# The softmax of a sliding-window attention in another order: upper parts before scaling, lower parts before scaling, biases one at a time

## The reference

```python
# first_block and the gMLP half of second_block come before; the part that the change touches:
def swa_mixer(h, k, v, w_in, sinks, w_out):
    q, z = jnp.split(h @ w_in, 2, axis=-1)
    q = q * (HEAD_DIM ** -0.5)
    ...
    dist = BLOCK + r - c
    in_window = (dist >= 0) & (dist < WINDOW)
    alibi = -slopes[:, :, None, None] * dist.astype(jnp.float32)
    def block_fn(args):
        ...
        logits = jnp.einsum('btkgd,bskd->bkgts', qb, kb).astype(jnp.float32) + alibi
        logits = jnp.where(valid, logits, -jnp.inf)
        m = jnp.maximum(jnp.max(logits, axis=-1), sink)
        p = jnp.exp(logits - m[..., None])
        denom = jnp.sum(p, axis=-1) + jnp.exp(sink - m)
        o = jnp.einsum('bkgts,bskd->btkgd', p.astype(vb.dtype), vb).astype(jnp.float32)
        return (o / denom.transpose(0, 3, 1, 2)[..., None]).astype(h.dtype)
    out = lax.map(block_fn, (jnp.arange(n_blocks), q_blocks))
    ...
    y = out * jax.nn.silu(z)
    return y @ w_out
```

## Time and profile before

| | us |
|---|---|
| median of 3 runs | 912.27 |
| lowest, highest | 911.54, 913.71 |
| profiled execution | 914.38 |
| span of its instructions | 912.6 |
| TensorE busy | 880.9 |
| GpSimd busy | 556.2 |
| VectorE busy | 548.0 |
| ScalarE busy | 357.8 |

### The profile page before, as it was taken

The page is one execution under the profiler, slowest core; times in us unless marked ns, Lnnn a source line. Parts: engine busy times, 40 slices in busy tenths (PEclk is TensorE's granted clock), DMA queues, the critical chain, the costliest instruction groups (busy, mean ns, idle before and its releaser), DMA issues.

```text
span 912.6 us, 11943 instructions
## 1 busy us (share of the span) xinstructions
PE 880.9 (97%) x4224; PEld 731.4 (80%) x4224; DVE 548.0 (60%) x878; ACT 357.8 (39%) x792; POOL 556.2 (61%) x620
## 2 busy tenths in 40 slices
PE   8999999999999989999999999999968999998997
PEld 6888888888888877888888888888848888776776
DVE  6125657774054589675745615568955376777734
ACT  5124333421143485554112411126434445756622
POOL 7766656567689731329973078752597795745352
PEclk9999999999999999999999999999997999999999
DMA  7443221242322647983832435239740222212102
GB/s 200 140 130 93 79 84 50 90 162 92 120 85 73 176 104 185 224 240 120 199 93 93 134 120 138 93 104 209 164 146 4 67 93 70 70 31 86 47 1 92
DMA packets 81516, 102.65 MB, mean 112 GB/s; under 512 B 11825, under 2 KB 54321, under 8 KB 81458
## 3 DMA queue, kind: packets, MB, share of 16 engines
q1 hardware_dynamic: 72752, 85.12, 29.3%
q0 software_dynamic: 8704, 16.78, 10.8%
q10 hardware_dynamic: 2, 0.00, 0.0%
HBM read 99.79 MB, written 2.10 MB: 112 GB/s over the span
## 4 chain that ended last, share of the span: by engine, by line
PE 82%; DVE 6%; POOL 5%; ACT 4%; issue 3%; POOLq 0%; DVEq 0%; ACTq 0%
PE bank L2027 25%; PE bank L2029 24%; PE bank L2028 24%; PE bank L2255 2%; PE bank L2111 1%; DVE pT L1979 1%; POOL wlo L843 1%; PE bank L2228 1%; DVE tok L1934 1%; POOL tok L813 1%; PE bank L2283 1%; POOL raw L813 1%; DVE den L1944 1%; POOL v5lo L843 1%; ACT pT L1351 1%
## 5 line engine op out<-in xcount | busy, mean ns | idle before, releaser
L843 POOL TENSOR_TENSOR wlo<-raw,whi 128x512 fp32r<-128x512 f32 x204 | 282.3, 1414 | 0.3 <-ACT whi L964 0.3
L836 POOL TENSOR_SCALAR whi<-raw 128x512 fp32r<-128x512 f32 x202 | 140.5, 732 | 198.8 <-PE bank L2029 189.8
L2027 PE MATMUL bank<-actB_hi,whi 128*128 128x512 f32 (+1 forms) x416 | 160.3, 385 | 2.3 <-POOL wlo L843 2.3
L2028 PE MATMUL bank<-actB_lo,whi 128*128 128x512 f32 (+1 forms) x416 | 159.4, 383 | 0.0
L2029 PE MATMUL bank<-actB_hi,wlo 128*128 128x512 f32 (+1 forms) x416 | 159.2, 383 | 0.0
L2027 PE MATMUL bank<-whi,actA_hi 128*128 128x512 f32 x320 | 128.1, 400 | 7.0 <-DVE wlo L1702 4.9
L2028 PE MATMUL bank<-wlo,actA_hi 128*128 128x512 f32 x320 | 125.7, 393 | 0.0
L2029 PE MATMUL bank<-whi,actA_lo 128*128 128x512 f32 x320 | 125.7, 393 | 0.0
L2027 PEld LDWEIGHTS bank<-actB_hi,whi 128*128 128x128 f32 x416 | 79.0, 190 | 17.4 <-issue 2.9
L2029 PEld LDWEIGHTS bank<-actB_hi,wlo 128*128 128x128 f32 x416 | 79.0, 190 | 15.1
L2028 PEld LDWEIGHTS bank<-actB_lo,whi 128*128 128x128 f32 x416 | 79.1, 190 | 14.2
(11 more groups left out here) (262 smaller groups left out, 1606.9 us busy)
## 6 DMA issues: line engine op xcount, KB each, us to landing
raw<-in_a_w_in SPq DMA_DIRECT2D x44, 512.0 KB, 4.4
raw<-in_w_in SPq DMA_DIRECT2D x32, 512.0 KB, 3.8
raw<-in_b_w_in SPq DMA_DIRECT2D x16, 512.0 KB, 3.4
raw<-in_a_w_out SPq DMA_DIRECT2D x12, 512.0 KB, 3.4
gain<-in_a_w_out POOLq DMA_DIRECT2D x9, 512.0 KB, 8.5
raw<-in_w_out SPq DMA_DIRECT2D x8, 512.0 KB, 3.8
raw<-in_w_ple_gate SPq DMA_DIRECT2D x8, 512.0 KB, 3.3
gain<-in_a_w_in POOLq DMA_DIRECT2D x8, 512.0 KB, 7.2
```

Of the source, the lines that this page charges most:

```text
L836: pool.tensor_scalar(H, src[:, i * HALF:(i + 1) * HALF], 1.0, 1.0, ALU.mult, ALU.mult).then_inc(w_hi, 1)
L843: ins = pool.tensor_tensor(L, src[:, i * HALF:(i + 1) * HALF], H.bitcast(f32), ALU.subtract)
L2027: M(out_, whi_, xhi_, start=start, stop=False)
L2028: M(out_, whi_, xlo_, start=False, stop=False)
```

## The change

In the loop of slots, three things stand in another order; nothing is added and nothing is left out.

- ScalarE: the copies of the upper parts (`pThi`, step i-2) come first in slot i, ahead of the scaling of step i-1 and the copy of the output of step i-3.
- VectorE: `probs2` is cut in two. `sums2` (sum and reciprocal of step i-1) comes first, then the lower parts (step i-2), then the scaling (step i-1), then the scores.
- VectorE: the biases of group 0 are made ahead of the loop. Those of group g > 0 are made one in each of the four slots of group g-1, behind the scores and the emptying of banks and ahead of the product with the gate. For groups 2 and 3, whose biases go where those of group 0 and 1 stood, a bias waits until the scores of that group are done.

```diff
--- before.py
+++ after.py
@@ -1332,6 +1332,10 @@
             for f in range(2):
                 q5_out(f)
             for i in range(SLOTS2 + 1):
+                for kt in ((0, 1) if STEPS2[i - 2][1] else (1,)) if 2 <= i < 18 else ():
+                    b = ("t5", i - 2, kt)
+                    act.wait_ge(pe_block, BLOCK[b])
+                    A(pThi(kt), psum[bank_of(b)][:, :], ACT.Copy).then_inc(pt_hi[kt], 1)
                 if 1 <= i < 17:
                     k0 = 0 if STEPS2[i - 1][1] else P
                     act.wait_ge(rec5, i)
@@ -1345,10 +1349,6 @@
                         A(o5[m * DH:(m + 1) * DH, 2 * g:2 * g + 2, b * P:(b + 1) * P],
                           psum[3][0:DH, :].rearrange("p (f m s) -> p m f s", f=2, m=2)[:, m], ACT.Copy)\
                             .then_inc(o5_copied, 1)
-                for kt in ((0, 1) if STEPS2[i - 2][1] else (1,)) if 2 <= i < 18 else ():
-                    b = ("t5", i - 2, kt)
-                    act.wait_ge(pe_block, BLOCK[b])
-                    A(pThi(kt), psum[bank_of(b)][:, :], ACT.Copy).then_inc(pt_hi[kt], 1)
                 for s, f in DONE2.get(i - 1, ()):
                     if s == "q5":
                         q5_out(f)
@@ -1920,10 +1920,6 @@
                 g, b = STEPS2[i]
                 k0 = 0 if b else P
                 if b == 0:
-                    dve.wait_ge(pe_block, BLOCK["v5", T - 1])
-                    for h in range(4):
-                        V.tensor_scalar(bias2(g)[:, h, :], dist2, -SLOPE2[4 * g + h], None, ALU.mult)\
-                            .then_inc(bias2_made, 1)
                     dve.wait_ge(bias2_made, 4 * g + 4)
                 if i >= 3:
                     dve.wait_ge(pe_block, BLOCK["t5", i - 3, 1])
@@ -1937,13 +1933,19 @@
                 dve.wait_ge(s5_scored, 4 * i + 4)
                 V.tensor_tensor(den[:, :], nmx[:, :], sinks[:, 4 * g:4 * g + 4], ALU.subtract).then_inc(sink5, 1)
 
-            def probs2(i):
-                g, b = STEPS2[i]
-                k0 = 0 if b else P
+            def make_bias2(g, h):
+                if g >= 2:
+                    dve.wait_ge(s5_scored, 16 * (g - 1))
+                V.tensor_scalar(bias2(g)[:, h, :], dist2, -SLOPE2[4 * g + h], None, ALU.mult).then_inc(bias2_made, 1)
+
+            def sums2(i):
                 dve.wait_ge(exp5, 5 * i + 5)
                 V.tensor_tensor(den[:, :], rs[:, :], esk[:, :], ALU.add).then_inc(den5, 1)
                 dve.wait_ge(den5, i + 1)
                 V.reciprocal(rr[:, :], den[:, :]).then_inc(rec5, 1)
+
+            def probs2(i):
+                k0 = 0 if STEPS2[i][1] else P
                 dve.wait_ge(rec5, i + 1)
                 for h in range(2):
                     pr = prob2(i)[:, h, k0:256]
@@ -1971,13 +1973,18 @@
             q5_rest(0)
             q5_rest(1)
             dve.wait_ge(dist_made, 4)
+            dve.wait_ge(pe_block, BLOCK["v5", T - 1])
+            for h in range(4):
+                make_bias2(0, h)
             for i in range(SLOTS2 + 1):
                 if 1 <= i < 17:
-                    probs2(i - 1)
+                    sums2(i - 1)
                 for kt in ((0, 1) if STEPS2[i - 2][1] else (1,)) if 2 <= i < 18 else ():
                     dve.wait_ge(pt_hi[kt], i - 1 if kt else kt0_steps(i - 2))
                     V.tensor_tensor(pTlo(kt), psum[bank_of(("t5", i - 2, kt))][:, :], pThi(kt).bitcast(f32),
                                     ALU.subtract).then_inc(pt_lo[kt], 1)
+                if 1 <= i < 17:
+                    probs2(i - 1)
                 if i < 16:
                     scores2(i)
                 for f in (f for s, f in DONE2.get(i - 1, ()) if s == "q5"):
@@ -1990,6 +1997,8 @@
                     dve.wait_ge(hi["y5"], f + 1)
                     V.tensor_tensor(actA_lo[:, f, :], acc[:, f % 2, :], actA_hi[:, f, :].bitcast(f32),
                                     ALU.subtract).then_inc(lo["y5"], 1)
+                if i < 12:
+                    make_bias2(i // 4 + 1, i % 4)
                 for f in (f for f in MEET2 if MEET2[f] == i):
                     if f >= 2:
                         dve.wait_ge(lo["y5"], f - 1)
```

## The result

| | before | after |
|---|---|---|
| median, us | 912.12 (4 runs) | 901.95 (4 runs, 901.45 to 902.77) |
| profiled execution | 914.38 | 902.16 |
| its span | 912.6 | 900.4 |

The ratio is 0.9887 with a 95% interval of 0.987 to 0.9904: 10.2 us at the median, where 902.1 was forecast.

A forecast was written before the change was run, and what follows sets the result against it. TensorE, busy 97% of the span, was taken as the bound; its waits 0.26 + 2.63 + 1.60 + 0.69 + 3.46 + 1.51 = 10.15 us came off the 912.27 median, giving 902.1, range 900.7 to 903.8, chance 0.70.

The forecast's parts named there:

- The bound: Second attention: TensorE waits for the lower parts in slots 9, 13 and 14, slightly in slot 5; 10.15 us could go.
- The 3.1 us of low clock: Slots 9 and 14: TensorE runs slowly behind the gaps at granted clock 0.56 and 0.50, costing 1.60 and 1.51 us.
- The round of the softmax: VectorE and ScalarE, second attention: a round takes 6.5 us in place of 7.9, about 5.5 in short slots.
- Which part gives it: Softmax round: upper parts first on ScalarE and lower parts before scaling on VectorE together shorten 7.9 us to 6.5.
- The biases: VectorE: 12 of 16 move behind the scores of slots 0 to 11, 0.28 to 1.38 us each, hidden by TensorE's spare time.
- The hardest place: Slot 12, VectorE's work taken as 4.49 us: slot 13's head 3.1 late, slot 14's bank reserve 0.5, no stall.
- A: Holds in slots 12 and 13 leave a 1.7 us gap in slot 14, 1.5 low clock behind: 905.3; chance 0.16.
- B: Slots 4, 8 and 12: late ScalarE heads make TensorE wait at the output bank, 12.75 us lost: 914.9; chance 0.03.
- C: Second attention: the 10 us are lost again to waits for weights, 912.3; chance 0.06.
- D: Gaps longer in timed runs, or small gaps hidden by modelled ends go too: about 899.5; chance 0.05.

## Why the prediction was right, point by point

- **The bound.** Waits of TensorE for the lower parts, removed: right. All of them went, and the attention shortened by 10.6 us against 10.15. Of the 0.46 between, slot 5 gives 0.34: I had counted only the visible 0.26 us of idle there, and from its first output product to the next slot's TensorE now needs 8.67 us in place of 9.27, 0.60 less.
- **The 3.1 us of low clock** (1.60 + 1.51) went with the gaps, as summed, in the traced execution. To take it off the median as well was luck in part: the gaps of 3.26 and 2.77 us in other kernels had no fall behind them, and the ten executions of the kernel before with a clock of 0.994 to 0.996 had less of it and were still 8.8 to 9.9 us slower than the changed kernel. How long their gaps were is open. In a kernel with such gaps this term is a likely one, not a fixed one, and that the forecast met the median to 0.2 us is better than the sum deserved.
- **The round of the softmax.** Forecast from the head H of a slot: lower parts H+0.63 to H+1.92, scores H+2.6, exponentials H+4.3, end H+6.5. Slot 7 of the kernel after, ScalarE:

```profile
782.28 1.09 ACT L1338 ACTIVATE pT<-bank 128x512 fp32r<-128x512 f32 x2 [1.07 <-PE bank L2292]
...
786.39 0.51 ACT L1365 ACTIVATE tok<-tok,nmx 128x256 f32<-128x256 f32 x1 [0.95 <-DVE nmx L1930]
...
788.38 0.19 ACT L1368 ACTIVATE esk<-den 128x4 f32<-128x4 f32 x1
```

  Exponentials at H+4.1, end at H+6.3: right to 0.2.
- **Which part gives it.** The prediction put the shorter round down to parts 1 and 2 together and gave part 2 (lower parts ahead of the scaling) a use of its own, "the lower parts start with the upper ones, not behind VectorE's own scaling". The runs show no such use: with the upper parts first, part 2 and its absence give the same time (901.6 against 901.9 and 902.5), since VectorE has its scaling done while it waits. Without part 1, part 2 is a loss of 0.85%. This step was wrong, and the total did not show it.
- **The biases.** That they are absorbed, one by one, was right; but with part 1 in place the block is absorbed too (902.59). Alone they are worth 0.7% (0.9929).
- **The hardest place.** Slot 12 was mis-sized. I kept the stretched 4.49 us of VectorE's work behind its scores; after, it took 2.30 (VectorE's timeline, the two rows are its start and end):

```profile
825.30 0.16 DVE L1934 TENSOR_TENSOR den<-nmx,sinks 128x4 f32<-128x4 f32 x1
...
827.60 0.56 DVE L1943 TENSOR_TENSOR den<-rs,esk 128x4 f32<-128x4 f32 x1
```

  T12, the end of slot 12's transposes, is 822.14 here. Slot 13's head (828.25) so came at T12+6.1, not 9.0, 0.2 us behind its transposes, not 3.1. The output copy ended 2.3 behind that head, not 2.8, since the scaling ahead of it is half as wide there (0.69 us). Slot 14 so had 3.7 us in reserve, not 0.5. The longest stretching had moved to slot 8, where the product took 1.76 us and the sum 1.25:

```profile
796.68 1.76 DVE L2007 SCALAR_TENSOR_TENSOR acc<-zg,o 128x512 f32<-128x512 f32 x1
798.36 1.25 DVE L1943 TENSOR_TENSOR den<-rs,esk 128x4 f32<-128x4 f32 x1
```

  Slot 9's head came 1.8 us behind its transposes (upper copy 799.01, transposes' end 797.24), where I had 1.2, and its reserve was over 2 as said (output copy's end at 801.3, asked for at 803.49). So stretched durations belong to a moment, not to a slot: the lower part, the product and the sum are stretched only where GpSimd works at the same time (counted in the last section).
- **The rivals.** A (a gap left at slot 14) did not come, by 3.7 us. B (the output bank) did not come in the changed kernel, but its mechanism was the first to bind when VectorE was loaded. C (weights) did not: GpSimd waited 46.0 us for TensorE, and TensorE for no weight in the attention. D (small hidden gaps go too) came in slot 5 alone, with 0.34 us.

## What to carry to other kernels

Where one engine waits and others run a chain in rounds, compare the length of one round with what the waiting engine needs for one slot, the short slots included; the chain's work that nobody waits for soon (here a scaling and a copy on ScalarE) is what to move behind. An edit that pulls a step ahead on one engine can be worth nothing or a loss when the step waits for another engine and something ready stands behind it: ask for each such move what its engine would have done in that wait. When two traces already differ ahead of the place of the change, find the wait behind which they part before anything is put down to the change. And time the parts of a change singly, since a right total can hold a part that gives nothing.

## What the runs showed of the hardware

- The granted clock fell behind gaps of 2.29, 2.63, 2.65, about 2.7, 2.76, 3.46 and 4.58 us and not behind 1.59, 2.19, 2.77 and 3.26; behind one wait of 1.7 us it fell in 3 traces of 14. In the two traces of the kernel before each fall in the attention took 1.5 to 1.65 us, and the one at 698 took 1.52.
- VectorE's small instructions with both operands in SBUF (lower part of the product, product, sum of four columns) and its biases are stretched only beside GpSimd's work. Counted over the attention in all 14 traces: the 48 products with no GpSimd row beside them took 0.68 or 0.69 us each, those beside one 0.68 to 1.78; the 87 sums without took 0.15 to 0.17, those beside one 0.14 to 1.32. The gate, which reads PSUM and one tensor in SBUF, took 0.67 to 0.69 every time, beside GpSimd too. The Trainium skill, SBUF — State Buffer, section "SBUF: two separate sides", has the ports that VectorE shares with GpSimd as an exclusive lock, for VectorE's instructions in a two-port mode or with two inputs in SBUF; which instructions were stretched here, and when, agrees with it. No run took GpSimd's work away to show it directly.
